# Retention stage of a float32 transformer kernel: value products and square sums laid between the gate blocks, rotations two blocks behind their projection

## The chip, the cores and the metric

The kernel runs on one core of one Trainium2 chip. The metric is the device time of one execution in microseconds (us); three runs of the kernel before gave 1600.77, 1602.77 and 1604.04, median 1602.77. The engines are TensorE (PE, with its weight loads as PEld), VectorE (DVE), ScalarE (ACT), GpSimd (POOL) and the DMA queue of SyncE (SP). Each works through its own instructions in order, and they wait for one another by semaphores.

## What is computed

The reference is two transformer blocks of two layers each on 256 tokens (16 meta tokens in front in the first), model width 1024, in float32: an attention with differential and grouped heads, a windowed attention, two squared-ReLU MLPs; then a retention layer, a mixture of experts, a block attention and a second mixture of experts. The change touches the retention layer alone, cut here to what matters (4 heads, key width 256, value width 512; the kernel computes the chunked recurrence as one decayed product, which is the same sum):

```python
def retention(x, w_in, w_out):
    proj = x @ w_in
    q, k, v, g = jnp.split(proj, [H * dk, 2 * H * dk, 2 * H * dk + H * dv], axis=-1)
    q = rotary(q, ...)
    k = rotary(k, ...) * (dk ** -0.5)
    # scores = (q k^T) * decay, causal; o = scores v, per head
    o = o * lax.rsqrt(jnp.mean(o * o, axis=-1, keepdims=True) + NORM_EPS)
    y = jax.nn.silu(g) * o
    return y @ w_out
```

## The kernel before, in words

Activations lie transposed, features on the partitions, tokens in the free dimension. Every large product is done as three products of float32r halves: a weight part of 128 x 1024 is copied to its high half by ACT (`weight_high`, L1808) and the rest is subtracted by DVE (`weight_low`, L2245); the activations are split in the same way into `x_high` and `x_low`. `three` (L1140 to L1142) issues low weight x high input, high weight x low input, high x high. There are four buffers for weight parts. `split_weights` splits part c only after TensorE has read part c-4, and `stay_ahead(key)` splits up to three parts beyond the block `key`; it stands at the head of each block on both ACT and DVE, so what is behind it in their programs waits until TensorE has come to the middle of that block.

The retention stage goes through TensorE in this order. Eight blocks `ret_qk` (L1492; 48 matmuls and two weight parts each; n = 0 to 3 queries, 4 to 7 keys), four blocks `ret_v` of four weight parts (L1507 to L1509), eight gate blocks `ret_g` (L1512), the scores of four heads `ret_s` (L1521), then per head h the value product `ret_o` (L1532, L1533) and, behind the value product of the next head, the sum of squares `ret_sq` (L1540), then eight blocks `ret_out` (L1140 to L1142 on `ret_high`, `ret_low`), with the router's first matmuls (L1550, L1552) before block 7. `take` waits until the PSUM banks of a result are drained; which banks a result gets and which engine drains it is planned at the head of the program (`plan_next`, `plan_columns`) in the order of TensorE.

DVE: `rotate(n)` (L2616 to L2622) reads block n from PSUM, multiplies by cosine and sine in `rtmp` and writes q or k. The rotations need the doubled normalisation (`doubly_normed`, L2590 to L2598), which is ready at block 2, so `rotate(0)`, `rotate(1)` and `rotate(2)` stand together there; behind block 4 comes `first_normed` (L2603 to L2606), which writes the first norm's result to `hT`. Gate blocks are drained and scaled in L2639, scores times decay are L2645 and L2646. Then per head: reciprocal of the root (L2652), scaling (L2654), product with the gate (L2655), and for the head before it the low parts of y (`low`, L2255).

ACT: it drains v (L1788) and applies silu to each gate block (L2092), then per head copies the value product from PSUM to `ro` (L2103), takes the root of the mean square (L1788, `drain`), squares into `rtmp` (L2112) and makes the high parts of y (`gated`, L2098).

Memory: `ro` lies over q and k, `ret_high` over the gates, `ret_low` over `x_high` and `x_low`, so that no low part of y can be written before the last gate block has read them. The root has two rows in `rms`, used in turn.

After the output projection the expert stage follows. Its weights are loaded by SP in order: into a dense tile's slot as soon as that tile has been split, into the last slots only when `ret_out` has ended.

Of the kernel before, what the change touches and what calls it, by code (L numbers as in the profile page):

```python
# [37 lines left out]
P = 128  # L38
# [122 lines left out]
def program(nc, A, out, dbg=None):  # L161
# [5 lines left out]
    def sem(name):  # L167
        return ctx.enter_context(nc.semaphore(name))
# [290 lines left out]
    for j in range(4):  # L459
        plan_next(("ret_v", j), "act", 2, parts=4)  # L460
        uses["ret_v", j]["quarter"] = len(quarters)
        for q in range(4):
            plan_quarter("ret_in", 4 + j, q, uses["ret_v", j]["full"] - 3 + q)
    for n in range(8):
        plan_columns("ret_g", n, "dve", 2, 8 + n // 2, 2 * (n % 2))
    for h in range(RET_H):
        plan_next(("ret_s", h), "dve")
    for h in range(RET_H + 1):
        if h < RET_H:
            plan_next(("ret_o", h), "act", 2)  # L470
        if h >= 1:
            plan_next(("ret_sq", h - 1), "act")
    turn[0] = 0
# [146 lines left out]
    SW = T0 + 1  # L620
    with nc.sbuf_tensor("ret_low", [P, 2 * KC, REAL], F32R) as yl:
        pass
    with nc.sbuf_tensor("ahead_a", [P, TILE], F32) as ahead_a:
# [229 lines left out]
    xh_ready, xl_ready = sem("xh_ready"), sem("xl_ready")  # L853
    ret_rot, ret_sT, ret_osq, ret_y = sem("ret_rot"), sem("ret_sT"), sem("ret_osq"), sem("ret_y")
    mmax, mexp, mprob = sem("mmax"), sem("mexp"), sem("mprob")
    raw_ready, raw_squared, rtok_sq, rtok_ready = sem("raw_ready"), sem("raw_squared"), sem("rtok_sq"), sem("rtok_ready")
# [265 lines left out]
    def _(pe):  # L1122
# [374 lines left out]
        for j in range(4):  # L1497
            take(("ret_v", j))
            b0, c0 = uses["ret_v", j]["banks"][0], uses["ret_v", j]["quarter"]
            for q in range(4):  # L1500
# [9 lines left out]
                mm.then_inc(psum_full, 1)  # L1510
        for n in range(8):
            columns(("ret_g", n), xhr, xlr, REAL)  # L1512
        pe.wait_ge(ret_rot, 8)
        got(("ret_v", 3))
        for h in range(RET_H):
# [7 lines left out]
            mm.then_inc(psum_full, 1)  # L1523
        for h in range(RET_H + 1):
            if h < RET_H:
                take(("ret_o", h))
                b0 = uses["ret_o", h]["banks"][0]
                pe.wait_ge(ret_sT, h + 1)
                for c in range(4):
                    o = psum[:, b0 + c // 2, REAL * (c % 2):REAL * (c % 2) + REAL]  # L1530
                    e = 512 * h + P * c
                    pe.matmul(o, rv[:, 0, e:e + P], rs_[:, h, 0:REAL], start=True, stop=True)  # L1532
                    mm = pe.matmul(o[:, P:REAL], rv[:, 1, e:e + P], rs_[:, h, REAL:384],  # L1533
                                   start=False, stop=True, skip_group_check=True)
                mm.then_inc(psum_full, 1)
            if h >= 1:
                o = take(("ret_sq", h - 1))
                pe.wait_ge(ret_osq, h)
                for c in range(4):
                    mm = pe.matmul(o[:, 0:REAL], const("ones"), rtmp[:, c, :], start=(c == 0), stop=(c == 3))  # L1540
                mm.then_inc(psum_full, 1)
        def router_scores(l, chunks):
# [229 lines left out]
    def _(act):  # L1772
# [316 lines left out]
        for n in range(8):  # L2089
            stay_ahead(("ret_g", n))  # L2090
            act.wait_ge(gate_scaled, n + 1)
            act.activation(rg[:, 2 * n:2 * n + 2, :], rg[:, 2 * n:2 * n + 2, :], ACT.Silu)  # L2092

# [5 lines left out]

        for h in range(RET_H + 1):  # L2100
            if h < RET_H:
                o = full(("ret_o", h)).rearrange("p b (c t) -> p (b c) t", c=2)
                act.activation(ro[:, 4 * h:4 * h + 4, :], o, ACT.Copy).then_inc(act_drained, 1)  # L2103
                act.wait_ge(act_drained, uses["ret_o", h]["drained"])
            if h >= 1:
                g = h - 1
                if g >= 2:
                    act.wait_ge(ret_y, g - 1)
                drain(("ret_sq", g), rms[:, g % 2, 0:REAL], lambda o: o[:, 0:REAL], ACT.Sqrt, bias=eps[:, 0:1],
                      scale=1.0 / 512)  # L2110
            if h < RET_H:
                act.activation(rtmp, ro[:, 4 * h:4 * h + 4, :], ACT.Square).then_inc(ret_osq, 1)  # L2112
            if h >= 2:
                gated(h - 2)
        gated(RET_H - 1)
        def router_squares(name, first):
# [103 lines left out]
    def _(v):  # L2220
# [402 lines left out]
        for n in range(8):  # L2623
            stay_ahead(("ret_qk", n))
            if n == 2:
                doubly_normed()
                rotate(0)
                rotate(1)
            if n >= 2:
                rotate(n)  # L2630
            if n == 4:
                first_normed()
        decay = const("decay", RET_H)
        for j in range(4):
            stay_ahead(("ret_v", j))
        for n in range(8):
            stay_ahead(("ret_g", n))
            o = full(("ret_g", n)).rearrange("p (c t) -> p c t", c=2)
            v.tensor_tensor(rg[:, 2 * n:2 * n + 2, :], o, rms[:, 1, 0:REAL].unsqueeze(1).to_broadcast([P, 2, REAL]),  # L2639
                            ALU.mult).then_inc(dve_drained, 1)  # L2640
            v.wait_ge(dve_drained, uses["ret_g", n]["drained"])
            v.sem_inc(gate_scaled, 1)
        for h in range(RET_H):
# [4 lines left out]
            v.sem_inc(ret_sT, 1)  # L2648
        for h in range(RET_H + 1):
            if h < RET_H:  # L2650
                drained_by_act(("ret_sq", h))
                link(v.reciprocal(rms[:, h % 2, 0:REAL], rms[:, h % 2, 0:REAL]))  # L2652
                y = ro[:, 4 * h:4 * h + 4, :]
                link(v.tensor_tensor(y, y, rms[:, h % 2, 0:REAL].unsqueeze(1).to_broadcast([P, 4, REAL]), ALU.mult))  # L2654
                v.tensor_tensor(y, y, rg[:, 4 * h:4 * h + 4, :], ALU.mult).then_inc(ret_y, 1)  # L2655
            if h >= 1:
                for c in range(4 * h - 4, 4 * h):
                    low("ret", c, ro, yh, yl)
        def router_input(key, l, c):
# [319 lines left out]
```

## Time and profile before

| | |
|---|---|
| median of three runs | 1602.77 us (1600.77 to 1604.04) |
| profiled execution | 1600.47 us |
| its span (first to last instruction) | 1598.6 us |
| mean granted clock of TensorE | 0.979 |
| busy share of the span: PE, PEld, DVE, ACT, POOL | 94%, 72%, 51%, 37%, 11% |
| v projection of the retention stage | 726.2 to 770.7 us |
| gate projection | 770.7 to 816.1 us |
| scores | 816.1 to 821.4 us |
| value products and square sums | 821.4 to 841.1 us |
| output projection | 841.1 to 895.1 us |

Times in the tables and rows are microseconds from the start of the span. A timeline's row gives start, duration, engine, line, operation, output and inputs, and in brackets how long the engine had been idle before it and who released it; rows of like instructions are merged, with their count behind an x. The granted clock is 1.00 at 2.4 GHz and 0.50 at 1.2 GHz.

### The profile page before, as it was taken

The page shows a single profiled execution, that of the slowest core. Times are in us where ns is not written, and L with a number is a line of the kernel's source. Part 1 is how long each engine was busy: PE and PEld are TensorE (multiplying, and loading weights), DVE is VectorE, ACT ScalarE, POOL GpSimd, SP SyncE. Part 2 cuts the span into 40 slices and gives each one's busy share as a digit, 9 for nine tenths or more (in the row PEclk, how much of TensorE's full clock was granted, in tenths as well). Part 3 has the DMA queues.
Part 4 walks back from the last instruction along what each step waited for, and adds up shares of the span by engine and source line. Part 5 has one row for each costly group of instructions (what it writes and reads, how often), then busy time and mean ns, then how long its engine had stood idle before and what let it go on. Part 6 is the DMA issues. An engine that isn't in the chain of part 4 may idle for free.

```text
span 1598.6 us, 25221 instructions
## 1 busy us (share of the span) xinstructions
PE 1507.7 (94%) x10010; PEld 1156.2 (72%) x10010; DVE 819.9 (51%) x1439; ACT 594.3 (37%) x1032; POOL 175.4 (11%) x171
## 2 busy tenths in 40 slices
PE   7998899998999999989999999899999999999997
PEld 6675899997679999988989844454676864444544
DVE  6877676677767656776557512112564542111213
ACT  4565444444664444534554211111333421111111
POOL 1000432243005322300000000000200000000000
PEclk9997999999999999999999999999999989999999
DMA  9041554544134545435421899999733189999993
GB/s 394 14 159 53 191 212 159 198 171 158 54 139 158 190 179 199 153 123 211 165 99 54 344 394 428 429 394 393 312 143 155 59 364 423 428 429 380 428 429 139
DMA packets 28761, 379.78 MB, mean 238 GB/s; under 512 B 3447, under 2 KB 4855, under 8 KB 5761
## 3 DMA queue, kind: packets, MB, share of 16 engines
q1 hardware_dynamic: 27312, 373.92, 58.3%
q0 software_dynamic: 928, 4.30, 0.8%
q8 instruction: 62, 1.02, 0.3%
q10 hardware_dynamic: 432, 0.32, 0.1%
q14 instruction: 27, 0.21, 0.0%
HBM read 377.45 MB, written 1.09 MB: 237 GB/s over the span
## 4 chain that ended last, share of the span: by engine, by line
PE 73%; DMA 11%; DVE 10%; ACT 3%; issue 2%; POOL 1%; SPq 0%; DVEq 0%; ACTq 0%; POOLq 0%
PE psum L1616 17%; PE psum L1140 12%; PE psum L1142 12%; PE psum L1141 12%; DMA ring<-w_expert_dram 11%; PE psum L1609 3%; PE psum L1168 2%; PE psum L1598 2%; DVE weight_low L2245 1%; PE psum L1509 1%; PE psum L1507 1%; PE psum L1508 1%; DVE x_low L2271 1%; PE psum L1437 1%; PE psum L1427 1%
## 5 line engine op out<-in xcount | busy, mean ns | idle before, releaser
L1140 PE MATMUL psum<-x_high,weight_low 128*128 128x256 f32 (+1 forms) x1184 | 349.9, 295 | 30.3 <-DVE weight_low L2245 14.9
L1142 PE MATMUL psum<-x_high,weight_high 128*128 128x256 f32 (+1 forms) x1184 | 339.6, 287 | 0.0
L1141 PE MATMUL psum<-x_low,weight_high 128*128 128x256 f32 (+1 forms) x1184 | 339.4, 287 | 0.0
L2245 DVE TENSOR_TENSOR weight_low<-ring,weight_high 128x1024 fp32r<-128x1024 f32 x196 | 254.9, 1309 | 120.3 <-ACT weight_high L1808 119.8
L1808 ACT ACTIVATE weight_high<-ring 128x1024 fp32r<-128x1024 f32 x196 | 205.3, 1054 | 160.3 <-PE psum L1142 132.1
L1140 PEld LDWEIGHTS psum<-x_high,weight_low 128*128 128x128 f32 x1184 | 226.4, 191 | 49.1 <-DVE weight_low L2245 17.9
L1141 PEld LDWEIGHTS psum<-x_low,weight_high 128*128 128x128 f32 x1184 | 226.4, 191 | 1.1 <-issue 0.7
L1142 PEld LDWEIGHTS psum<-x_high,weight_high 128*128 128x128 f32 x1184 | 226.8, 192 | 0.0
L1616 PE MATMUL psum<-ring,xn 128*64 128x512 f32 x832 | 187.6, 607 | 14.8 <-DMA ring<-w_expert_dram 14.5
L1616 PEld LDWEIGHTS psum<-ring,xn 128*64 128x64 f32 x832 | 66.1, 140 | 133.8 <-issue 133.8
L1140 PE MATMUL psum<-hidden_high,weight_low 128*128 128x272 f32 (+1 forms) x512 | 145.7, 285 | 1.3 <-DVE hidden_low L2467 1.3
L1141 PE MATMUL psum<-hidden_low,weight_high 128*128 128x272 f32 (+1 forms) x512 | 145.7, 285 | 0.0
L1142 PE MATMUL psum<-hidden_high,weight_high 128*128 128x272 f32 (+1 forms) x512 | 145.5, 284 | 0.0
L1616 PE MATMUL psum<-ring,arena 128*64 128x512 f32 x576 | 127.6, 595 | 0.0
L2807 DVE TENSOR_TENSOR arena<-arena,psum 128x512 f32<-128x512 f32 x18 | 12.4, 688 | 216.3 <-PE psum L1616 216.3
L2459 DVE TENSOR_TENSOR weight_low<-ring,weight_high 128x1024 fp32r<-128x1024 f32 x64 | 87.2, 1362 | 60.7 <-ACT weight_high L1981 60.7
L1140 PEld LDWEIGHTS psum<-hidden_high,weight_low 128*128 128x128 f32 x512 | 96.1, 188 | 1.6 <-DVE hidden_low L2467 1.6
L1142 PEld LDWEIGHTS psum<-hidden_high,weight_high 128*128 128x128 f32 x512 | 96.6, 189 | 0.0
L1141 PEld LDWEIGHTS psum<-hidden_low,weight_high 128*128 128x128 f32 x512 | 96.3, 188 | 0.0
L1086 POOL TENSOR_TENSOR xn<-xn 128x256 f32<-128x256 f32 (+1 forms) x35 | 36.2, 1036 | 532.4 <-ACT xn L1844 499.3
L1616 PEld LDWEIGHTS psum<-ring,arena 128*64 128x64 f32 x576 | 39.7, 137 | 74.1 <-issue 72.0
L1981 ACT ACTIVATE weight_high<-ring 128x1024 fp32r<-128x1024 f32 x64 | 67.7, 1058 | 57.4 <-PE psum L1142 57.4
(354 smaller groups left out, 2405.7 us busy)
## 6 DMA issues: line engine op xcount, KB each, us to landing
ring<-w_expert_dram SPq DMA_DIRECT2D x88, 2048.0 KB, 14.6
ring<-w_dense_dram SPq DMA_DIRECT2D x68, 2048.0 KB, 7.8
ahead_a<-w_expert_dram SPq DMA_DIRECT2D x10, 2048.0 KB, 15.3
arena<-w_expert_dram SPq DMA_DIRECT2D x10, 2048.0 KB, 19.6
arena<-scratch_dram POOLq DMA_DIRECT2D x1, 3328.0 KB, 13.1
constants_sb<-constants_dram SPq DMA_DIRECT2D x1, 1287.5 KB, 7.5
hT<-x_dram SPq DMA_DIRECT2D x1, 1088.0 KB, 5.2
constants_sb<-constants_dram SPq DMA_DIRECT2D x1, 1056.0 KB, 15.8
```

Of the source, the lines that this page charges most:

```text
L1086: pool.tensor_tensor(part[:, 0, :], part[:, 0, :], part[:, c, :], ALU.add).then_inc(folded, 1)
L1140: pe.matmul(o, wl[:, c % 4, cols], high, start=start, stop=False)
L1141: pe.matmul(o, wh[:, c % 4, cols], low, start=False, stop=False)
L1142: return pe.matmul(o, wh[:, c % 4, cols], high, start=False, stop=stop)
L1168: mm = pe.matmul(o[0:b - a, 0:n], x[:, k, a:b], w[:, k, first:first + n], start=(k == 0), stop=(k == KC - 1))
L1598: mm = pe.matmul(psum[:, 4 + c // 2, REAL * (c % 2):REAL * (c % 2) + REAL], part[:, c * P:(c + 1) * P], oht[:, :], start=False, stop=done ...
L1609: mm = pe.matmul(psum[:, c // 4, P * (c % 4):P * (c % 4) + P], xnat[:, tt, c * P:(c + 1) * P], oh[:, tt, :], start=(tt == 0), stop=(tt == 1))
L1616: mm = pe.matmul(psum[HALF * x:HALF * x + HALF, bank, :], x_[:, k, HALF * x:HALF * x + HALF], w[x][:, k, cols], start=start, stop=stop)
L1808: act.activation(split_view(wh, (name, j), c), quarter_view((name, j), q), ACT.Copy).then_inc(wh_ready, 1)
L1981: act.activation(split_view(wh, key, m["quarter"] + x), quarter_view(key, x % 4), ACT.Copy).then_inc(wh_ready, 1)
L2245: v.tensor_tensor(split_view(wl, (name, j), c), quarter_view((name, j), q), split_view(wh, (name, j), c).bitcast(F32), ALU.subtract).then_ ...
L2459: v.tensor_tensor(split_view(wl, key, c), quarter_view(key, x % 4), split_view(wh, key, c).bitcast(F32), ALU.subtract).then_inc(wl_ready, 1)
```

## The change

Of the plan and of TensorE's program: the scores are moved ahead of the gate blocks; the value product of head n stands behind gate block n (n = 0 to 3), the square sum of head n-1 between gate block n and that value product (n = 1 to 4); gate blocks 5 to 7 follow alone. On DVE rotation n-2 stands at block n, rotations 6 and 7 at v blocks 0 and 1, the first norm at v block 2; the decay products come before the gate blocks; per head, reciprocal and scaling (`scaled`) are parted from the product with the gate (`gate`) and from the low parts (`lows`), and all of them are laid between the gate blocks' drains. On ACT the copies, roots and squares are laid between the weight parts of the gate blocks, and the silus are gathered from block 5 on. The root keeps one row, guarded by a new semaphore `ret_scaled`; `gate_done` counts the silus. `ret_low` is moved to the place of v, which is dead after the last value product.

```diff
+    for h in range(RET_H):
+        plan_next(("ret_s", h), "dve")
     for n in range(8):
         plan_columns("ret_g", n, "dve", 2, 8 + n // 2, 2 * (n % 2))
-    for h in range(RET_H):
-        plan_next(("ret_s", h), "dve")
-    for h in range(RET_H + 1):
-        if h < RET_H:
-            plan_next(("ret_o", h), "act", 2)
-        if h >= 1:
-            plan_next(("ret_sq", h - 1), "act")
+        if 1 <= n <= RET_H:
+            plan_next(("ret_sq", n - 1), "act")
+        if n < RET_H:
+            plan_next(("ret_o", n), "act", 2)
...
-    with nc.sbuf_tensor("before_gate", [P, GATE_AT], F32):
-        with nc.sbuf_tensor("ret_high", [P, 2 * KC, REAL], F32R) as yh:
+    with nc.sbuf_tensor("before_low", [P, GATE_AT - 2 * KC * REAL], F32):
+        with nc.sbuf_tensor("ret_low", [P, 2 * KC, REAL], F32R) as yl, \
+             nc.sbuf_tensor("ret_high", [P, 2 * KC, REAL], F32R) as yh:
...
+        for n in range(8):
+            columns(("ret_g", n), xhr, xlr, REAL)
+            if 1 <= n <= RET_H:
+                ret_square(n - 1)
+            if n < RET_H:
+                ret_values(n)
...
+        for n in range(8):
+            stay_ahead(("ret_g", n))
+            if 1 <= n <= RET_H:
+                if n >= 2:
+                    act.wait_ge(ret_scaled, n - 1)
+                drain(("ret_sq", n - 1), rms[:, 0, 0:REAL], lambda o: o[:, 0:REAL], ACT.Sqrt, bias=eps[:, 0:1],
                       scale=1.0 / 512)
+            if n < RET_H:
+                o = full(("ret_o", n)).rearrange("p b (c t) -> p (b c) t", c=2)
+                act.activation(ro[:, 4 * n:4 * n + 4, :], o, ACT.Copy).then_inc(act_drained, 1)
+                act.wait_ge(act_drained, uses["ret_o", n]["drained"])
+                act.activation(rtmp, ro[:, 4 * n:4 * n + 4, :], ACT.Square).then_inc(ret_osq, 1)
+            if n == 5:
+                for m in range(5):
+                    silu(m)
+            if n >= 6:
+                silu(n - 1)
+            if n == 7:
+                gated(0)
+                gated(1)
+        silu(7)
+        stay_ahead(("ret_out", 0))
+        gated(2)
+        stay_ahead(("ret_out", 1))
+        gated(3)
...
             stay_ahead(("ret_qk", n))
             if n == 2:
                 doubly_normed()
-                rotate(0)
-                rotate(1)
             if n >= 2:
-                rotate(n)
-            if n == 4:
-                first_normed()
+                rotate(n - 2)
         decay = const("decay", RET_H)
         for j in range(4):
             stay_ahead(("ret_v", j))
+            if j < 2:
+                rotate(6 + j)
+            if j == 2:
+                first_normed()
...
+        def scaled(h):
+
+            drained_by_act(("ret_sq", h))
+            link(v.reciprocal(rms[:, 0, 0:REAL], rms[:, 0, 0:REAL]))
+            y = ro[:, 4 * h:4 * h + 4, :]
+            v.tensor_tensor(y, y, rms[:, 0, 0:REAL].unsqueeze(1).to_broadcast([P, 4, REAL]), ALU.mult).then_inc(ret_scaled, 1)
+
+        def gate(h):
+
+            v.wait_ge(gate_done, 2 * h + 2)
+            v.wait_ge(ret_scaled, h + 1)
+            y = ro[:, 4 * h:4 * h + 4, :]
+            v.tensor_tensor(y, y, rg[:, 4 * h:4 * h + 4, :], ALU.mult).then_inc(ret_y, 1)
+
+        def lows(h):
+
+            for c in range(4 * h, 4 * h + 4):
+                low("ret", c, ro, yh, yl)
+
+        for n in range(8):
+            stay_ahead(("ret_g", n))
+            if n == 7:
+                lows(0)
+                lows(1)
+            o = full(("ret_g", n)).rearrange("p (c t) -> p c t", c=2)
+            v.tensor_tensor(rg[:, 2 * n:2 * n + 2, :], o, rms[:, 1, 0:REAL].unsqueeze(1).to_broadcast([P, 2, REAL]),
+                            ALU.mult).then_inc(dve_drained, 1)
+            v.wait_ge(dve_drained, uses["ret_g", n]["drained"])
+            v.sem_inc(gate_scaled, 1)
+            if 2 <= n <= 5:
+                scaled(n - 2)
+            if n == 6:
+                gate(0)
+                gate(1)
+            if n == 7:
+                gate(2)
+        stay_ahead(("ret_out", 0))
+        gate(3)
+        lows(2)
+        lows(3)
```

## Rows read from the trace of the kernel before

**Rows 1.** The page, part 1: busy time, share of the span, instructions.
```profile
PE 1507.7 (94%) x10010; PEld 1156.2 (72%) x10010; DVE 819.9 (51%) x1439; ACT 594.3 (37%) x1032; POOL 175.4 (11%) x171
```
**Rows 2.** Windows: stretch, length, busy PE, PEld, DVE, ACT, POOL, clock, DMA share, GB/s.
```profile
698.20:726.20 28.00, 21.70 (x170) 21.30 (x169) 27.65 (x54) 7.42 (x7) 0.00 (x0) 0.94 0.33 114
726.20:770.70 44.50, 44.50 (x194) 36.14 (x193) 22.80 (x24) 19.71 (x19) 0.00 (x0) 1.00 0.57 212
770.70:816.10 45.40, 45.40 (x385) 45.38 (x384) 24.45 (x23) 22.81 (x25) 0.00 (x0) 1.00 0.50 185
816.10:821.40 5.30, 5.30 (x35) 4.89 (x34) 2.84 (x7) 0.63 (x1) 0.00 (x0) 1.00 0.01 3
841.10:895.10 54.00, 51.12 (x420) 50.89 (x418) 33.39 (x44) 18.29 (x25) 0.00 (x0) 0.97 0.30 115
...
983.00:1072.00 89.00, 82.19 (x442) 39.77 (x442) 14.73 (x30) 12.56 (x15) 0.00 (x0) 0.98 1.00 426
```
**Rows 3.** Timeline of PE around the gap in the query and key projections.
```profile
698.11 0.28 PE L1142 MATMUL psum<-x_high,weight_high 128*128 128x256 f32 x1
703.88 0.58 PE L1140 MATMUL psum<-x_high,weight_low 128*128 128x256 f32 x1 [5.49 <-DVE weight_low L2245]
704.26 0.41 PE L1141 MATMUL psum<-x_low,weight_high 128*128 128x256 f32 x1
...
717.62 0.39 PE L1140 MATMUL psum<-x_high,weight_low 128*128 128x256 f32 x1 [0.81 <-DVE weight_low L2245]
```
**Rows 4.** Timeline of DVE: first rotation, the next low parts, the first norm's scalings.
```profile
695.85 0.42 DVE L2616 TENSOR_TENSOR arena<-psum,arena 128x256 f32<-128x256 f32 x1
...
702.61 2.35 DVE L2245 TENSOR_TENSOR weight_low<-ring,weight_high 128x1024 fp32r<-128x1024 f32 x2
...
713.17 3.25 DVE L2606 SCALAR_TENSOR_TENSOR hT<-hT,gains_sb,arena 128x256 f32<-128x256 f32 x8
```
**Rows 5.** PE from the first value product on (timeline); router matmuls in 880 to 892 (by line).
```profile
821.37 0.60 PE L1532 MATMUL psum<-xn,arena 128*128 128x256 f32 x2
...
826.61 1.89 PE L1540 MATMUL psum<-arena,constants_sb 128*128 128x256 f32 x8
828.34 0.59 PE L1532 MATMUL psum<-xn,arena 128*128 128x256 f32 x2
...
839.51 1.97 PE L1540 MATMUL psum<-arena,constants_sb 128*128 128x256 f32 x8 [1.74 <-ACT arena L2112]
...
845.77 0.39 PE L1140 MATMUL psum<-ret_high,weight_low 128*128 128x256 f32 x1 [2.88 <-DVE ret_low L2255]
...
L1552 PE MATMUL psum<-router,xn x16: 266/266/266, 885.9 to 889.2; 128*128 128x20 f32 x16
```
**Rows 6.** Timeline of ACT: silu, weight part, table load, root, high parts; the router's root.
```profile
811.43 0.63 ACT L2092 ACTIVATE arena<-arena 128x512 f32<-128x512 f32 x1 [2.50 <-DVEq L2642]
811.97 1.04 ACT L1808 ACTIVATE weight_high<-ring 128x1024 fp32r<-128x1024 f32 x1
...
828.60 1.28 ACT L1788 ACT_TABLE_LOAD   x1 [0.77 <-PE psum L1540]
829.90 0.47 ACT L1788 ACTIVATE rms<-psum,eps 128x256 f32<-128x256 f32 x1
...
834.86 1.32 ACT L2098 ACTIVATE ret_high<-arena 128x256 fp32r<-128x256 f32 x4
...
900.78 0.20 ACT L2132 ACTIVATE small<-small 128x2 f32<-128x2 f32 x1 [4.01 <-DVE small L2681]
```
**Rows 7.** Timeline of DVE: gate drain, reciprocal, scaling, low parts of a head.
```profile
816.33 0.69 DVE L2639 TENSOR_TENSOR arena<-psum,rms 128x512 f32<-128x512 f32 x1 [0.46 <-PE psum L1142]
...
830.40 1.75 DVE L2652 RECIPROCAL rms<-rms 128x256 f32<-128x256 f32 x1 [8.08 <-ACT rms L1788]
832.19 1.23 DVE L2654 TENSOR_TENSOR arena<-arena,rms 128x1024 f32<-128x1024 f32 x1
...
844.29 1.42 DVE L2255 TENSOR_TENSOR ret_low<-arena,ret_high 128x256 fp32r<-128x256 f32 x4
```
**Rows 8.** Timeline of SP: issue of an expert tile behind the output projection.
```profile
896.57 0.55 SPq L978 DMA_DIRECT2D ahead_a<-w_expert_dram  x1
```

More of the change, by code:

```diff
@@ L620, in program @@
     SW = T0 + 1
-    with nc.sbuf_tensor("ret_low", [P, 2 * KC, REAL], F32R) as yl:
-        pass
     with nc.sbuf_tensor("ahead_a", [P, TILE], F32) as ahead_a:
@@ L854, in program @@
     ret_rot, ret_sT, ret_osq, ret_y = sem("ret_rot"), sem("ret_sT"), sem("ret_osq"), sem("ret_y")
+    ret_scaled, gate_done = sem("ret_scaled"), sem("gate_done")
     mmax, mexp, mprob = sem("mmax"), sem("mexp"), sem("mprob")
@@ L1510, in _ @@
                 mm.then_inc(psum_full, 1)
-        for n in range(8):
-            columns(("ret_g", n), xhr, xlr, REAL)
         pe.wait_ge(ret_rot, 8)
-        got(("ret_v", 3))
         for h in range(RET_H):
@@ L1523, in _, with ret_square, ret_values @@
             mm.then_inc(psum_full, 1)
[L1524 to L1541, printed above, removed]
+        def ret_square(h):
+            o = take(("ret_sq", h))
+            pe.wait_ge(ret_osq, h + 1)
+            for c in range(4):
+                mm = pe.matmul(o[:, 0:REAL], const("ones"), rtmp[:, c, :], start=(c == 0), stop=(c == 3))
+            mm.then_inc(psum_full, 1)
+        def ret_values(h):
+            take(("ret_o", h))
+            if h == 0:
+                got(("ret_v", 3))
+            b0 = uses["ret_o", h]["banks"][0]
+            pe.wait_ge(ret_sT, h + 1)
+            for c in range(4):
+                o = psum[:, b0 + c // 2, REAL * (c % 2):REAL * (c % 2) + REAL]
+                e = 512 * h + P * c
+                pe.matmul(o, rv[:, 0, e:e + P], rs_[:, h, 0:REAL], start=True, stop=True)
+                mm = pe.matmul(o[:, P:REAL], rv[:, 1, e:e + P], rs_[:, h, REAL:384],
+                               start=False, stop=True, skip_group_check=True)
+            mm.then_inc(psum_full, 1)
+        for n in range(8):
[4 more added lines that the diff above has]
+                ret_values(n)
         def router_scores(l, chunks):
@@ L2088, in _, with silu @@
             drain(("ret_v", j), rv[:, :, 512 * j:512 * j + 512], lambda o: o)
-        for n in range(8):
-            stay_ahead(("ret_g", n))
+        def silu(n):
             act.wait_ge(gate_scaled, n + 1)
-            act.activation(rg[:, 2 * n:2 * n + 2, :], rg[:, 2 * n:2 * n + 2, :], ACT.Silu)
+            act.activation(rg[:, 2 * n:2 * n + 2, :], rg[:, 2 * n:2 * n + 2, :], ACT.Silu).then_inc(gate_done, 1)
         def gated(g):
@@ L2098, in gated @@
                 act.activation(yh[:, c, :], ro[:, c, :], ACT.Copy).then_inc(xh_ready, 1)
[L2100 to L2109, printed above, removed]
-                      scale=1.0 / 512)
[L2111 to L2115, printed above, removed]
+        for n in range(8):
[4 more added lines that the diff above has]
+                drain(("ret_sq", n - 1), rms[:, 0, 0:REAL], lambda o: o[:, 0:REAL], ACT.Sqrt, bias=eps[:, 0:1],
+                      scale=1.0 / 512)
+            if n < RET_H:
[16 more added lines that the diff above has]
+        gated(3)
         def router_squares(name, first):
@@ L2635, in _ @@
             stay_ahead(("ret_v", j))
[L2636 to L2642, printed above, removed]
+            if j < 2:
+                rotate(6 + j)
+            if j == 2:
+                first_normed()
         for h in range(RET_H):
@@ L2648, in _ @@
             v.sem_inc(ret_sT, 1)
[L2649 to L2658, printed above, removed]
+        def scaled(h):
[32 more added lines that the diff above has]
+        lows(3)
         def router_input(key, l, c):
```

## Prediction

> **What bounds the kernel now.** I read the page first, for which engine is full: TensorE is busy 94% of the span [rows 1], so a microsecond counts only if it is one in which TensorE stands still or runs slow. Next I cut the retention stage at TensorE's boundaries [rows 2]. The reader is to see that in 698.2 to 726.2 and in 841.1 to 895.1 PE is busy for less than the stretch and the granted clock is under 1.00, while the v and g projections (44.5 and 45.4 us) have neither. Then I read PE's timeline in those places, and in the stretch of the value products between them, for the time lost, and the timelines of DVE and ACT for what TensorE was waiting for.
>
> *Query and key projections.* The last matmul before the gap starts at 698.11; at the pace of 0.118 us per matmul (a g block is 45.4 / 8 = 5.675 us for 48 of them [rows 2]) its next slot is 698.23. TensorE resumes at 703.88, 5.65 us late, waiting for a low weight part, and then runs at half clock for a while (0.41 us long instead of 0.28; granted clock 0.94 over the stretch) [rows 2, 3]. Seven half blocks of 2.84 us follow the gap, so the stage would end at 698.23 + 19.87 = 718.1; it ends at 726.2. **8.1 us** are lost: 5.65 gap, 0.81 at 717.62 [rows 3], the rest slow clock (about 1.4) and a small wait. The cause is in DVE's rows: rotations 0, 1 and 2 stand in a row from 695.85, (702.61 - 695.85) / 3 = 2.25 us each, and only then come the two low parts that TensorE needs first [rows 4]. Later the first norm (a reciprocal of 1.75 as in [rows 7] and 3.25 us of scalings at 713.17 [rows 4]) cuts in again, which makes the 0.81.
>
> *Values.* From 821.37 to 841.1 TensorE does four value products, (826.61 - 821.37) / 2 = 2.62 us each, and four square sums, 828.34 - 826.61 = 1.73 each, together 17.4 us in 19.7 [rows 2, 5]: **2.3** lost, of which 1.74 wait for the last square [rows 5].
>
> *Output projection.* 841.1 to the end of block 7 at 895.1 is 54.0 us. Its work is 45.4 like that of the g projection (as many matmuls of the same form), and 3.6 for the router's first matmuls between blocks 6 and 7 [rows 5], 49.0. **5.0** lost: 3.0 until 845.77 for the low parts of head 1 (2.88 by the row), which stand on DVE behind head 2's scaling and gating, and about 2 at half clock after it (granted clock 0.97 over the stretch) [rows 2, 5, 7]. So 8.1 + 2.3 + 5.0 = 15.4 us can be won; the matmuls stay the same.
>
> **The change part by part.** *Rotations two blocks behind, first norm moved into the v stage.* No instruction is added. DVE starts rotation 0 at 695.85 as now and ends it at 698.1; the low weight part behind it (2.35 / 2 = 1.18 [rows 4]) lands at 699.3. TensorE is 1.1 late instead of 5.65. From there DVE needs two low parts and one rotation per block, 4.6 us against 5.675 of TensorE, and gains on it: the next parts land at 700.5, 703.9, 705.1, 708.5 and are needed at 702.2, 705.0, 707.8, 710.7. The gap of 0.81 is followed by matmuls 0.39 us long and then by full speed up to the v projection; the clock then does not halve for long, so I charge nothing for it, bound 1.4, the price after the long gap. The v projection starts at 719.2, **7.0 earlier**. Rotations 6 and 7 and the first norm go where DVE is busy 22.8 of 44.5 us [rows 2]; the norm holds the last low part of the v stage back by about 3.5, and it is then still ready some 2.5 before its use. Without that cover it costs up to 5.
>
> *Scores before the gate blocks.* The same 32 matmuls, 821.4 - 816.1 = 5.3 us [rows 2]. Rotation 7 is ready some 20 us before. DVE's decay products keep TensorE's pace as now, and only value product 0, one gate block later, waits for them. Nought, with a whole block (5.7) as cover.
>
> *Value products and square sums between gate blocks.* Take the start of gate block 0 as 0. TensorE's work is 45.4 + 4 x 2.62 + 4 x 1.73 = 62.8 us; blocks 1 to 3 last 10.0 each. Per head ACT does a copy and a square (1.04 each, 1024 columns like a weight part), a root 0.47 and two weight parts [rows 6]; DVE does a reciprocal 1.75, a scaling 1.23, the gate drain 0.69 [rows 7] and two low parts. New waits: ACT's root of head h waits until DVE has scaled head h-1 (one row of the root tile is left), and behind it on ACT stand the copy and square of head h+1, for which the next square sum waits, and the next weight parts, for which DVE and then TensorE wait. One turn (drain 0.7, reciprocal and scaling 3.0, root 0.5, copy 1.0, square 1.0, weight part 1.0, low part 1.2, handoffs of under 0.1) is about 9 us, under 10.0. Carried through by hand: DVE ends the scaling of heads 0 to 3 at 28.0, 38.0, 48.0 and 55.7; gate blocks 4 to 7 end at 44.0, 51.4, 57.1 and 62.8 if TensorE never waits. The low parts for the second halves of blocks 6 and 7 land at 50.8 and 56.9 and are needed at 54.3 and 59.9. So no wait, with 3 us to spare.
>
> The end is tighter. ACT: weight parts to 50.45, table load 1.28, five silus 0.54 apart to 54.6, weight parts to 56.5, silu 5, a weight part at 57.3 and one at 60.05, silu 6, the high parts of heads 0 and 1 (1.32 each [rows 6]) to 64.0. DVE: low parts to 51.9, drain 5, scaling 3 to 55.7, low parts to 58.05, drain 6, gatings 0 and 1 (1.23 each) to 61.1, two low weight parts to 63.4, the low parts of head 0 (1.42 for four [rows 7]) to 64.8 and of head 1 to 66.1. For the first of these the output projection waits: it starts at 64.8 instead of 62.8, **2.0 late**, and finds head 1 ready 1.4 later. Against 2.3 + 5.0 lost now that is **5.3 earlier**. In this stage a gap of 1.74 left PE's pace as it was, one of 3.0 did not [rows 5]; 2.0 is nearer to the first, so no charge for the clock, bound 2. If each of the twelve handoffs from 44 on costs 0.1 more, that is 1.2; what ACT or DVE does faster gives back at most the 2.0.
>
> *Low parts in the values' place.* Free in itself: heads 0 and 1 can be split while gate block 7 still reads x high and low, as assumed above. Otherwise they would follow the block and add their 2.8. The root's table load leaves the way of the first root (828.60 [rows 6]); one comes back before the router's root, where ACT stood idle 4.01 us before 900.78 [rows 6], so hidden, else 1.3. Heads 2 and 3 are finished under output blocks 0 and 1; the nearest weight part, for the second half of block 2, lands about 1.0 before its use.
>
> On the table switch a rule speaks against my sum. The load at 828.60 lasts 1.28 and the root starts 0.02 after it [rows 6]. The Trainium skill (ScalarE: Activation LUTs, What ACT_TABLE_LOAD costs) gives a switch a drain besides, 2.66 us in all. By it ACT's five silus would end 1.4 later, DVE's next low part would wait for them, and the output projection would start at 66.2 instead of 64.8. The row shows no such drain behind the load, and I take the row.
>
> *Sum.* 7.0 + 5.3 = 12.3 us. It passes on to the end: the expert stage is DMA bound (share 1.00, 426 GB/s in 983 to 1072 [rows 2]), but its loads are issued as the output projection frees its tiles, and the last right behind its end (896.57 [rows 8]), so they move with it. Profiled execution: 1600.47 - 12.3 = 1588.2. The median of the three runs is 2.3 above the profiled one; against it 1602.77 - 12.3 = **1590.5**, my forecast.
>
> **The rivals.** *A, the tail of the gate stage binds harder.* The gap before the output projection is 3.3 instead of 2.0 and the clock halves after it, 2 more: 1602.77 - 12.3 + 3.3 = 1593.8; with the clock's 1.4 after the first gap 1595.2. For it: half clock after both long gaps. Against it: none after 1.74.
> *B, only the rotations pay.* The loop of ACT and DVE takes back all that the new order gives: 1602.77 - 7.0 = 1595.8. It needs 5.3 us more lateness, where I find 3 to spare.
> *C, slower.* The handshake through the single root row. If a turn takes longer than TensorE's 10.0 us, four turns wait for the difference, with all that queues behind ACT's wait. It turns the sum over when four turns exceed 40 by 3 spare plus 12.3, turns of about 14; at 15 the time is 1590.5 + 20 - 3 = 1607.5. Against it: each operation in the loop has a row, and they add up to 9.
> *D, the expert weights give it back.* 1602.8, if a transfer did not move with the stage. Against it: the issue times [rows 8].
> *E, nearly all gaps close.* 1602.77 - 15.4 = 1587.4.
>
> **How the numbers follow.** Forecast (1588.3 to 1592.7) 0.55; A 0.19; B 0.06; C 0.05; D 0.04; E and a little better 0.11. About 0.2%, 3.2 us, is what a measurement of this kernel can tell from no change. Faster: forecast, A, B, E, 0.91; same: D, 0.04; slower: C, 0.05. The range takes in E, A and B with 1.8 us on either side for the spread of three runs: 1585.5 to 1597.5.
>
> **What would show it.** Right: from the first gap on, the q and k projections with one wait of about 1 us at clock 1.00; square sums and values directly behind the gate blocks; one wait of about 2 us for a low part of head 0 before the output projection; from the last v matmul to the end of output block 7 about 119 us instead of 124.4. Wrong: waits for low weight parts within gate blocks 4 to 7 (B, C); a clock under 1.00 after a gap (A); longer DMA waits in the expert stage (D). I am likeliest to be wrong in the tail, where ACT and DVE hand work to each other without spare time.

## The result, and the profile after

| | before | after |
|---|---|---|
| median, runs of the first comparison | 1603.14 us (6) | 1592.99 us (6) |
| ratio, 95% interval | | 0.9933 (0.992 to 0.9946) |
| ratio in two later comparisons | | 0.993 (0.9906 to 0.9953), 0.9934 (0.9916 to 0.9952) |
| profiled execution | 1600.47 us | 1591.45 us |
| its span | 1598.6 us | 1589.6 us |
| mean granted clock | 0.979 | 0.977 |

The kernel became 10 to 12 us faster. The median forecast was 1590.5 us; the three comparisons gave 1592.99, 1590.79 and 1591.76, the first of them 0.3 us above the band of 1588.3 to 1592.7 that the forecast stood for. The forecast of 12.3 us is a ratio of 0.9923, which lies inside all three intervals; the profile shows all the same that one stretch of the sum, the output projection, fell short by 2 us. The page's first part, as in [rows 1]:

```profile
PE 1511.2 (95%) x10010; PEld 1160.5 (73%) x10010; DVE 819.0 (52%) x1439; ACT 593.4 (37%) x1032; POOL 173.4 (11%) x171
```

The same instructions, the same work, a shorter span. The windows at TensorE's boundaries of the kernel after (stretch, length, busy PE, PEld, DVE, ACT, POOL, clock, DMA share, GB/s; beside [rows 2]) are: from the end of the first wait of the query projection, v, scores, gate blocks with all square sums and values, output projection.

```profile
700.50:721.30 20.80, 19.94 (x168) 19.94 (x169) 19.67 (x35) 7.42 (x7) 0.00 (x0) 1.00 0.55 203
721.30:765.80 44.50, 44.50 (x194) 36.22 (x194) 30.21 (x43) 19.73 (x19) 0.00 (x0) 1.00 0.48 176
765.80:771.00 5.20, 5.20 (x34) 4.76 (x32) 2.15 (x6) 1.97 (x2) 0.00 (x0) 1.00 0.27 117
771.00:834.10 63.10, 63.06 (x483) 61.23 (x481) 38.02 (x35) 31.00 (x40) 0.00 (x0) 1.00 0.36 132
834.10:888.70 54.60, 52.70 (x416) 52.73 (x417) 30.81 (x46) 19.59 (x30) 0.00 (x0) 0.94 0.31 119
...
876.00:879.00 3.00, 3.00 (x30) 3.00 (x28) 1.31 (x3) 0.63 (x1) 0.00 (x0) 1.00 0.82 328
879.00:882.00 3.00, 3.00 (x18) 3.00 (x18) 0.00 (x0) 0.00 (x0) 0.00 (x0) 0.56 0.98 421
882.00:885.00 3.00, 3.00 (x16) 3.00 (x16) 0.00 (x0) 0.00 (x0) 0.00 (x0) 0.50 1.02 431
885.00:888.00 3.00, 3.00 (x22) 3.00 (x22) 0.00 (x0) 0.00 (x0) 0.00 (x0) 0.80 0.36 153
```

PE is busy without a break from 701.4 through gate block 7; the clock is 1.00 there. What is left stands in the last window and in the four rows below it: the output projection begins with a wait, and 3 us after the first of the router's narrow matmuls (876.4) the granted clock is halved for about 7 us, in which most of block 7 runs. TensorE's waits between 680 and 889, in all of them (who waited for whom, us in total, times, longest):

```profile
PE psum L1139 <- DVE ret_low L2272: 1.9, 1, 1.9
PE psum L1139 <- DVE weight_low L2262: 0.9, 1, 0.9
```

Where the time came from, each stretch measured at the same matmuls in both profiles. The marks are the first matmul of the query projection behind its 1.47 us wait, the first v matmul, the first matmul of the output projection, and the first of the routing's transposes behind it:

| stretch | before | after | forecast |
|---|---|---|---|
| query projection to v | 59.21 | 52.12 | -7.0 |
| v to output projection | 114.88 | 114.65 | -0.3 |
| output projection to the transposes | 59.19 | 56.24 | -5.0 |
| sum | 233.28 | 223.01 (-10.27) | -12.3 |
| transposes to the end of the span | 698.29 | 697.36 | 0 |

Up to the query projection the profile after lies 2.2 us later than the one before (669.23 and 667.03), in code that was not touched. In further profiles of the same kernel it lies at 667.09 and 667.39, so that is the spread of an execution.

### The profile page after: what moved, and what is told of

It is laid out like the page before. It is cut to its first block, busy times and chain, and to the rows that moved or that the text cites. A ratio compares the mean times of both kernels' runs of the same rounds, so it can differ in the third digit from the quotient of the medians.

```text
span 1589.6 us, 25224 instructions
## 1 busy us (share of the span) xinstructions
PE 1511.2 (95%) x10010; PEld 1160.5 (73%) x10010; DVE 819.0 (52%) x1439; ACT 593.4 (37%) x1032; POOL 173.4 (11%) x171
## 4 chain that ended last, share of the span: by engine, by line
PE 74%; DMA 11%; DVE 9%; ACT 2%; issue 1%; POOL 1%; SPq 0%; DVEq 0%; ACTq 0%; POOLq 0%
PE psum L1624 17%; PE psum L1139 13%; PE psum L1141 12%; PE psum L1140 12%; DMA ring<-w_expert_dram 11%; PE psum L1617 2%; DVE weight_low L2262 2%; PE psum L1167 2%; PE psum L1606 2%; PE psum L1508 1%; PE psum L1506 1%; PE psum L1507 1%; DVE x_low L2288 1%; PE psum L1436 1%; PE psum L1426 1%
## 5 line engine op out<-in xcount | busy, mean ns | idle before, releaser
L2262 DVE TENSOR_TENSOR weight_low<-ring,weight_high 128x1024 fp32r<-128x1024 f32 x196 | 255.0, 1313 | 119.1 <-ACT weight_high L1816 118.5
```

The costliest lines, as they stand in the source:

```text
L2262: v.tensor_tensor(split_view(wl, (name, j), c), quarter_view((name, j), q), split_view(wh, (name, j), c).bitcast(F32), ALU.subtract).then_ ...
```

## The experiments

The times are medians, compared with the kernel before on the same chip in the same set. The first set had a median of 1603.09 us for the kernel before, the second 1602.92, the third 1602.55.

**The changed kernel once more** (no edit).

> The changed kernel once more, unaltered, to see which of its features recur in a second profile. Theory 1 (the gain falls short of 12.3 us because the granted clock halves once in the output projection, at the router's narrow matmuls before block 7, which costs about 3.0 us): the half clock is there again, and from the first matmul of the output projection to the end of block 7 it takes about 52.6 us again. Theory 2 (where the clock halves is chance, as it was in 160 to 240 us, where the two profiles also differ): 49 to 50 us this time, or the half clock elsewhere. Time about 1593 either way.

1590.79 us, 12.3 below the kernel before, ratio 0.993. The three stretches of the table took 52.25, 114.66 and 55.51 us. The half clock was there again, 3.3 us after the first of the router's narrow matmuls, for about 3.5 us instead of 7:

```profile
874.00:877.00 3.00, 3.00 (x30) 3.00 (x28) 1.30 (x3) 0.63 (x1) 0.00 (x0) 1.00 0.82 322
877.00:880.00 3.00, 3.00 (x19) 3.00 (x19) 0.00 (x0) 0.00 (x0) 0.00 (x0) 0.61 1.02 437
880.00:883.00 3.00, 3.00 (x23) 3.00 (x23) 0.00 (x0) 0.00 (x0) 0.00 (x0) 0.83 1.02 431
```

Theory 1 holds as to the place, but its price does not: the output projection to the end of block 7 took 51.2 us, not 52.6 again. The slow stretch was half as long, and it cost about half as much.

**Rotations alone.** The kernel before, with DVE's order of the change:

```diff
             if n == 2:
                 doubly_normed()
-                rotate(0)
-                rotate(1)
             if n >= 2:
-                rotate(n)
-            if n == 4:
-                first_normed()
+                rotate(n - 2)
...
             stay_ahead(("ret_v", j))
+            if j < 2:
+                rotate(6 + j)
+            if j == 2:
+                first_normed()
```

> The kernel before with one part of the change: rotations two blocks behind, the first norm at v block 2. By the prediction's sum: first wait about 0.9 instead of 5.5 us, v projection 7 us earlier, values and output projection as before, time 7.0 us below the kernel before (ratio 0.9956). If the rotations only move the wait (DVE full in the v stage): less than 3 us.

1595.82 us, 7.3 below, ratio 0.9951 (0.9936 to 0.9967). TensorE's waits from 680 to 890:

```profile
PE psum L1140 <- DVE ret_low L2255: 2.9, 1, 2.9
PE psum L1540 <- ACT arena L2112: 2.1, 2, 1.7
PE psum L1140 <- DVE weight_low L2245: 0.9, 1, 0.9
```

The wait of 5.5 [rows 3] is down to 0.9, those of the values stand as before [rows 5]. DVE is not full in the v stage: it is busy 30.2 of 44.5 us there, where it was 22.8 before [rows 2].

**Values alone.** The changed kernel with the rotations back in place:

```diff
             if n == 2:
                 doubly_normed()
+                rotate(0)
+                rotate(1)
             if n >= 2:
-                rotate(n - 2)
+                rotate(n)
+            if n == 4:
+                first_normed()
...
             stay_ahead(("ret_v", j))
-            if j < 2:
-                rotate(6 + j)
-            if j == 2:
-                first_normed()
```

> The changed kernel with the rotations and the first norm back in their old places: only the order of values, square sums and low parts is new. By the sum of the prediction 5.3 us below the kernel before (ratio 0.9967), with the gap of 5.5 us back in the query and key projections and one wait of about 2 us before the output projection. If the half clock in block 7 belongs to the new order, about 2.5 to 3 us below. If the two parts were not additive (one hides the other's wait) the two times would not sum to the whole change's 10.15 us.

1599.19 us, 3.9 below, ratio 0.9983 (0.9969 to 0.9997). Waits:

```profile
PE psum L1139 <- DVE weight_low L2262: 6.3, 2, 5.5
PE psum L1139 <- DVE ret_low L2272: 1.9, 1, 1.9
```

The two parts add up: 7.3 + 3.9 = 11.2, between the 10.15 and the 12.3 of the whole. The values' part is the one that falls short of its sum (5.3, where the interval reaches from 0.5 to 5.0). The expectation had set 5.3 without a half clock in block 7 against 2.5 to 3 with it; 3.9 lies between and does not decide. From the output projection to the transposes this kernel took 55.50 us, again with a half clock behind the router's matmuls.

**Low parts in their old place.** DVE waits for the end of gate block 7 before it writes them:

```diff
+    with nc.sbuf_tensor("ret_low", [P, 2 * KC, REAL], F32R) as yl:
+        pass
     with nc.sbuf_tensor("ahead_a", [P, TILE], F32) as ahead_a:
...
             if n == 7:
+                v.wait_ge(psum_full, uses["ret_g", 7]["full"])
                 lows(0)
                 lows(1)
```

> The changed kernel with the low parts of y back over x high and x low, so that DVE waits for the end of gate block 7 before it writes them. In the changed kernel DVE comes to them 0.5 us after that end anyway, so by my theory the place is worth nothing here: same time as the changed kernel within 0.3 us, wait before the output projection still 1.9 us. If the new place carries part of the gain, 1 to 3 us slower. The pace of the matmuls in the output projection (120.0 ns apart in the changed kernel, 118.5 in the one before) goes back to 118.5 if it hangs on where the low parts lie, worth 0.6 us.

1591.45 us against 1590.79, no difference that a measurement shows, and the wait is 1.9 as in the changed kernel. The new place allows an earlier start that the change does not use. But it has a price that I had put at nothing. Ten microseconds inside the output projection, all at clock 1.00, no wait; first the kernel before, then after, then this one (the number behind PE's busy time counts the matmuls in the window, those cut by its edges too):

```profile
857.00:867.00 10.00, 10.00 (x87) 10.00 (x86) 5.68 (x6) 4.04 (x4) 0.00 (x0) 1.00 0.34 143
```
```profile
857.00:867.00 10.00, 10.00 (x85) 10.00 (x85) 5.67 (x7) 3.81 (x5) 0.00 (x0) 1.00 0.01 2
```
```profile
857.00:867.00 10.00, 10.00 (x87) 10.00 (x86) 5.81 (x8) 4.77 (x5) 0.00 (x0) 1.00 0.01 2
```

Over some 280 matmuls each, the starts lie 118.5, 120.0 and 118.5 ns apart. 384 matmuls by 1.5 ns is 0.6 us. Between the second and the third only the address of the low parts differs, and the wait on DVE that goes with it, which is long over in this window.

**The tail in another order.** To test what the 1.94 us before the output projection hang on:

```diff
         for n in range(8):
+            if n == 7:
+                split_weights(uses["ret_g", 7]["quarter"] + 4)
+                gated(0)
+                gated(1)
             stay_ahead(("ret_g", n))
...
-            if n == 7:
-                gated(0)
-                gated(1)
...
         for n in range(8):
-            stay_ahead(("ret_g", n))
             if n == 7:
                 lows(0)
                 lows(1)
+            stay_ahead(("ret_g", n))
...
         lows(2)
-        lows(3)
...
         for n in range(8):
             stay_ahead(("ret_out", n))
+            if n == 1:
+                lows(3)
```

> The changed kernel with the tail of the gate stage in another order: at gate block 7 ACT makes the high parts of heads 0 and 1 between its two weight parts instead of behind both, DVE makes the low parts of these heads before its two low weight parts instead of behind them, and the low parts of head 3 come one output block later. If the 1.94 us wait before the output projection is DVE's queue (two low weight parts, 2.35 us, ahead of the low parts of head 0), it goes to 0.3 or less and the time falls by 1.6 to 1.9 us against the changed kernel run again (1590.79), with no new wait for weight parts in output blocks 1 to 3. If it is ACT's chain (gating, high parts) that ends last, the wait stays at about 1.9.

1588.87 us, ratio 0.9912 (0.9896 to 0.9928). DVE's timeline in the changed kernel and in this one:

```profile
829.89 2.36 DVE L2672 TENSOR_TENSOR arena<-arena 128x1024 f32<-128x1024 f32 x2 [0.22 <-DVE arena L2685]
832.17 2.35 DVE L2262 TENSOR_TENSOR weight_low<-ring,weight_high 128x1024 fp32r<-128x1024 f32 x2
834.44 2.76 DVE L2272 TENSOR_TENSOR ret_low<-arena,ret_high 128x256 fp32r<-128x256 f32 x8
```
```profile
829.88 2.36 DVE L2673 TENSOR_TENSOR arena<-arena 128x1024 f32<-128x1024 f32 x2 [0.22 <-DVE arena L2686]
832.16 2.77 DVE L2273 TENSOR_TENSOR ret_low<-arena,ret_high 128x256 fp32r<-128x256 f32 x8
834.85 2.35 DVE L2263 TENSOR_TENSOR weight_low<-ring,weight_high 128x1024 fp32r<-128x1024 f32 x2
```

The gatings end at 832.2 in both. With the two low weight parts (2.35) behind the eight low parts of y instead of ahead of them, TensorE goes from gate block 7 into the output projection at 833.90 with no wait; of TensorE's waits only the first 0.9 is left, and from v to the output projection it takes 112.55 instead of 114.65. Here the new place of the low parts is used: DVE starts them 1.9 us before gate block 7 has ended. The edit moves two things at once. ACT makes its first high part at 831.14 instead of 832.81, and without that DVE could not have begun at 832.16; what DVE's order is worth alone was not run.

**The same, with the rotations three blocks behind.**

```diff
             if n == 2:
                 doubly_normed()
-            if n >= 2:
-                rotate(n - 2)
+            if n >= 3:
+                rotate(n - 3)
...
             stay_ahead(("ret_v", j))
-            if j < 2:
-                rotate(6 + j)
+            if j == 0:
+                rotate(5)
+                rotate(6)
+            if j == 1:
+                rotate(7)
```

> The same with the rotations three blocks behind their projection, so that the low weight parts of block 3 come before rotation 0. The first wait of 0.9 us is the rotation's 2.25 us minus what TensorE still has in hand; with three blocks it is gone: query and key projections 0.9 to 1.0 us shorter, time 2.5 to 2.9 below the changed kernel. If the doubled normalisation before it is the limit, the wait stays.

1590.51 us, ratio 0.9921 (0.9905 to 0.9936): not lower than the tail alone, though TensorE has no wait at all left between 680 and 880 and the query and key projections took 50.98 us. In the profile the time is lost again behind them: from the output projection to the transposes 56.17 us, where the tail alone took 53.66. Three microseconds a row, around block 7, first the tail alone, then both:

```profile
877.00:880.00 3.00, 3.00 (x27) 3.00 (x27) 0.00 (x0) 0.00 (x0) 0.00 (x0) 1.00 1.01 431
880.00:883.00 3.00, 3.00 (x27) 3.00 (x27) 0.00 (x0) 0.00 (x0) 0.00 (x0) 1.00 1.02 437
```
```profile
872.83:875.83 3.00, 3.00 (x21) 3.00 (x21) 0.00 (x0) 0.00 (x0) 0.00 (x0) 0.70 1.01 431
875.83:878.83 3.00, 3.00 (x16) 3.00 (x16) 0.00 (x0) 0.00 (x0) 0.00 (x0) 0.50 0.98 421
```

**The router's first matmuls behind block 7.** In the changed kernel:

```diff
         for n in range(8):
-            if n == 7:
-                pe.wait_ge(small_loaded, 48)
-                take(("logit", 0))
-                router_scores(0, range(4))
...
+        pe.wait_ge(small_loaded, 48)
+        take(("logit", 0))
+        router_scores(0, range(4))
```

> The changed kernel with the router's first sixteen matmuls of 20 columns and sixteen of 1 column moved from before output block 7 to behind it. Theory 1 (the narrow matmuls bring the granted clock down, and block 7 behind them pays): block 7 runs at clock 1.00, 5.7 us long instead of 7.4 to 8.6, and the time is up to 2 us below the changed kernel, less what these matmuls then cost in front of the routing (nothing while they cover VectorE's last residual, about 2 us). Theory 2 (the clock falls there by chance of place, not for the narrow matmuls): it falls in block 7 or elsewhere as often, and the time is the same or up to 2 us longer.

1591.91 us, ratio 0.9926 (0.9911 to 0.994). Block 7 ran at full clock, and the clock fell behind it:

```profile
876.20:879.20 3.00, 3.00 (x27) 3.00 (x27) 0.00 (x0) 0.01 (x1) 0.00 (x0) 1.00 0.99 426
879.20:882.20 3.00, 3.00 (x29) 3.00 (x28) 1.55 (x2) 0.85 (x2) 1.63 (x2) 1.00 1.02 437
882.20:885.20 3.00, 3.00 (x26) 3.00 (x27) 1.02 (x5) 1.27 (x2) 0.60 (x2) 0.91 1.01 431
885.20:888.20 3.00, 3.00 (x15) 3.00 (x16) 0.00 (x0) 0.00 (x0) 0.00 (x0) 0.50 1.00 426
```

The output projection to the transposes took 55.72 us, as in the changed kernel (55.51 to 56.24). So theory 1 fits as to what comes first (narrow matmuls, then the low clock) and is wrong about the worth of moving them: the second half of the narrow matmuls and the transposes then run slow themselves. The time alone is what theory 2 had forecast, the same or up to 2 us longer.

**All three edits.**

> The three edits together: tail reordered, rotations three behind, router's matmuls behind block 7. If the waits are independent: 4 to 5 us below the changed kernel (about 1586), from the start of the query and key projections to the end of output block 7 about 214 us less the router's 3.6. If the clock's fall only moves behind block 7, 2.5 to 3 below.

1588.99 us, ratio 0.9917 (0.9902 to 0.9932): 51.04, 112.56 and 55.79 us for the three stretches. That is 1.8 below the changed kernel of the first set (1590.79), less than either expectation. The waits are gone, the clock's share is not.

**Third set, all on one chip.** The rotations three blocks behind without the tail (the same edit of DVE's order, on the changed kernel), and three kernels again without an edit of their own: the changed kernel, the tail, both.

> The changed kernel with the rotations three blocks behind, the tail as in the change. If the wait of 0.9 us is worth its length: from the first matmul of the query and key projections to the v projection 51.0 instead of 52.1 us, and about 1 us below the changed kernel in the median, which five rounds hardly tell from no change. If the time saved is lost to the clock or to the v stage: as the changed kernel.

> The changed kernel a third time, on the same chip as the others of this set: the gain in the median, 10.15 and 12.3 us so far, between these two. The clock halves around the router's matmuls before block 7 in this profile too if it belongs to them; if it is left to chance, it is missing in about one profile of four, as so far (6 of 8 kernels with these matmuls before block 7 showed it).

> The reordered tail once more, beside the changed kernel on the same chip: 1.9 us below it if the removed wait counts in full; its first profile had no half clock before block 7, so its profile may be 2 us longer this time while the median stays 1.9 below.

> Tail and rotations three blocks behind once more, beside both alone: 2.9 us below the changed kernel if both waits count in full; if the first result (1.6 above the tail alone) was not noise, again above the tail alone.

| kernel | median | ratio, interval | query to v | v to output | output to transposes |
|---|---|---|---|---|---|
| rotations three behind | 1591.8 | 0.9926 (0.9904 to 0.9948) | 50.94 | 114.66 | 57.76 |
| changed kernel | 1591.76 | 0.9934 (0.9916 to 0.9952) | 52.15 | 114.67 | 56.23 |
| tail | 1588.61 | 0.9912 (0.9889 to 0.9936) | 52.11 | 112.55 | 53.90 |
| both | 1589.94 | 0.9918 (0.9902 to 0.9935) | 51.14 | 112.55 | 56.75 |

The changed kernel stays at 10.8 below the kernel before. The tail is 3.15 below the changed kernel in the median, in the profiles 2.1 for the wait and 2.3 for a clock that does not fall in block 7. Over all sets, each run taken against its set's kernel before, the means of the two kernels differ by 3.0 us, give or take 2.1 (two standard errors).

The rotations three blocks behind save their 1.0 to 1.3 us in each of the four profiles (50.94 to 51.14 against 52.11 to 52.30), and in the median nothing that these runs can tell: both edits together lie 1.4 above the tail alone over the two sets, give or take 2.1. In the profiles of this set the stretch to the transposes is 1.5 us longer with them than in the changed kernel beside it (with them the clock fell behind the 1.94 us wait as well), and 2.9 longer in both edits than in the tail alone.

The changed kernel had its half clock in or just before block 7 in three profiles of three, both edits together in two of two, the tail alone in none of two. That looks like a property of each kernel; seven profiles do not rule out chance.

## Why the prediction was right, point by point

The two waits left, their places and their lengths came out as forecast (0.86 us against 1.1, 1.94 against 2.0). One of the signs named for it did not: from the last v matmul to the end of output block 7 it took 123 us (765.8 to 888.75), not 119. The difference is in the output projection, below.

*Query and key projections, 7.0.* Measured 7.09 in the profile (59.21 - 52.12), 7.3 in the median of the rotations alone. The stretch varies by 1.4 us with the slow clock at its very start (50.74 in two other profiles with the same wait), which no edit touched. The wait was forecast at 1.1 and is 0.86; nothing was charged for the clock, and it stayed at 1.00. The timeline of PE, at its only wait before the output projection:

```profile
701.36 0.39 PE L1139 MATMUL psum<-x_high,weight_low 128*128 128x256 f32 x1 [0.86 <-DVE weight_low L2262]
```

*Scores, no cost.* 5.2 us in a row behind v, as before [rows 2].

*Gate stage, start of the output projection 64.8 us after gate block 0.* That block starts at 771.0 and the output projection at 836.00: 65.0. The hand schedule held at each step. DVE ended the scalings at 28.1, 38.1, 48.1 and 55.7 (forecast 28.0, 38.0, 48.0, 55.7) and the low parts of head 0 at about 64.8. No gate block waited for a weight part, so rivals B and C, the loop through the single root row, are out: ACT did wait there, 5.6 us for each of three roots, but nothing of TensorE's stood behind it in time.

```profile
819.22 0.47 ACT L1796 ACTIVATE rms<-psum,eps 128x256 f32<-128x256 f32 x1 [5.56 <-DVE arena L2665]
819.60 2.00 ACT L1816 ACTIVATE weight_high<-ring 128x1024 fp32r<-128x1024 f32 x2
821.61 1.28 ACT L2100 ACT_TABLE_LOAD   x1
822.90 2.72 ACT L2100 ACTIVATE arena<-arena 128x512 f32<-128x512 f32 x5
```

The first silu starts 0.01 us after the end of the table load. The drain that the Trainium skill (ScalarE: Activation LUTs, What ACT_TABLE_LOAD costs) adds to a switch is not there; with its 1.4 us the wait before the output projection would, by the prediction's own sum, have been 3.3, and it is 1.94.

*Rival A, half.* The gap before the output projection was 1.94 to 1.95 us, and in five of the seven profiles with it the clock stayed at 1.00 behind it, the changed kernel's three among them. In the other two it fell (low parts in the old place: 0.63 and 0.80 in the first two stretches of 3 us; rotations three behind: 0.52 and 0.91). So the bound of 2 us that I kept open was a true one, and that nothing was to be charged in the changed kernel's profiles was luck as much as reason.

*Output projection, 5.0: the term that was mis-sized.* I took its work as 45.4 + 3.6 = 49.0 us and let it run at full clock. From its first matmul to the end of block 7 it took 52.75 in the changed kernel (836.00 to 888.75), 3.7 more. Two things are missing from the sum. One is the pace of 120.0 ns, 0.6 us, which comes from the new place of the low parts; putting them back took it away. The other is the half clock behind the router's matmuls, the remaining 3.1, which the profile of the kernel before did not have in block 7 and I therefore did not put in. The tail alone, at the same pace and without that half clock, took 49.6 us for it in both profiles, which leaves these 3.1. Part of it came back at once: the kernel before had its slow clock behind block 7 instead and took 5.25 us from there to the transposes (895.06 to 900.31), the changed one 3.5 (888.75 to 892.24). So the stretch to the transposes shows 56.24, 55.51 and 56.23 in three profiles where the sum gives 59.19 - 5.0 = 54.2, and the 1.3 to 2.0 us by which the profiles fall short of the sum are accounted for.

That the slow block 7 belongs to the new order is not shown: the old order of the values with the new rotations had it as well (882.9 to 889.7, block 7 at 884.9 to 892.8; 61.72 us for the stretch against 59.19, part of it from a slow clock twice as long behind the 2.9 us wait). One profile of the kernel before was without it; how often its timed executions have it stays open, and with that which part of the spread 10.15, 12.3 and 10.8 is the clock's.

*Passing on to the end; rival D.* From the transposes to the end of the span it took 698.29 before, and 697.36, 699.09 and 697.86 in the three profiles after. So the expert weights moved with the stage. In the other experiments this stretch, which none of them edits, spread from 697.9 to 702.8, so the whole time of one profile cannot judge an edit worth 1 to 2 us.

*Rival E* needed all waits gone. The tail's reordering and the rotations three blocks behind reach that, and 1588.6 to 1590.5 in the median against its 1587.4.

## What to carry to other kernels

When work is laid into the gaps of a long product, follow the queue of each helper engine by hand through the last blocks: here the middle had 3 us to spare, and the longer of the two waits left, 1.94 us, stood in the order of a few items in the queues of DVE and ACT, where what TensorE needs next must stand ahead of what it needs one block later. A sum against one profile takes over that profile's luck with the clock, so take a second one before believing a difference of 2 us. The version with the reordered tail (ratio 0.9912 twice) is the fastest measured; its lead over the changed kernel, 3.0 us give or take 2.1, is small against the spread.

## What the runs showed of the hardware

The granted clock fell to half 2.5 to 3.7 us after the first of the router's narrow matmuls (1 and 20 columns), on an engine without an idle gap there: 9 of the 12 profiles with these matmuls before block 7 show it in or just before that block, for about 3.5 or 7 us. In the changed kernel the stretch to the transposes is 1.6 to 2.6 us longer than in the tail alone, which has no half clock before the end of block 7. With the narrow matmuls behind block 7 it fell behind block 7. An edit that moved the stage by 1.1 us went with its return in a kernel that was without it, in both of its profiles. That the narrow matmuls bring it about is the likeliest reading and not shown: in three of the 12 profiles the same matmuls were not followed by it before block 7 had ended. The expert weights' transfers do not decide it: their share of the DMA engines is 1.0 in block 7 of the tail alone as well, at clock 1.00.

The same float32r matmuls start 118.5 or 120.0 ns apart, depending on where in the same memory their low input lies: 118.5 in the three profiles with the old place, 120.0 in the eleven with the new one. What in the address decides it was not tried.
